# ScalarE and VectorE in place of GpSimd for the weight split of the plain projection stages

## What is computed

```python
def _ab_mixer(h, pos, s0, k_past, v_past, w_in, w_out, lam, lam_init, g_diff):
    qa, ka, va, ga, qb, kb, vb = jnp.split(h @ w_in, _cuts(AB_WIDTHS), axis=-1)
    qa = _rotary(qa.reshape(B, L, H_A, DK_A), pos)
...
def _gla_mixer(h, s0, w_in, w_gate, b_gate, g_norm, w_out):
    q, k, v, r, a = jnp.split(h @ w_in, _cuts(C_WIDTHS), axis=-1)
```

## Time and profile before

| | |
|---|---|
| median of 3 runs | 3545.07 us (3543.67 to 3548.8) |
| profiled execution | 3540.22 us |
| its span, first to last instruction | 3538.4 us |
| mean granted clock of TensorE | 0.940 of full speed |
| busy: PE / DVE / ACT / POOL | 3037.2 / 1540.1 / 1030.3 / 375.0 us |

### The profile page before, as it was taken

One profiled execution on the slowest core, in us unless ns is written; L12 is line 12 of the kernel. 1 busy time (PEld: TensorE's weight loads), 2 busy tenths in 40 slices (PEclk: granted clock), 3 DMA queues, 4 the chain that ended last, 5 costly groups with the idle time before them and its releaser, 6 DMA issues. The chain is left out here.

```text
span 3538.4 us, 52416 instructions
## 1 busy us (share of the span) xinstructions
PE 3037.2 (86%) x19700; PEld 2801.0 (79%) x19700; DVE 1540.1 (44%) x2144; ACT 1030.3 (29%) x1907; POOL 375.0 (11%) x281
## 2 busy tenths in 40 slices
PE   4699986788699999999984999767489999999996
PEld 2688874344499999999984989556288999999996
DVE  2144113556556444444446000287628444444545
ACT  4111111334444233322325101243225332333222
POOL 1212100000200000000001223163100000000000
PEclk8899997899799999999997999889789999999998
DMA  4354533775331111111103211121223111111113
GB/s 164 113 183 170 177 132 113 278 258 191 103 115 53 46 43 42 41 41 48 43 26 106 78 58 66 40 77 36 97 97 125 47 43 41 47 41 47 41 41 103
DMA packets 154186, 319.76 MB, mean 90 GB/s; under 512 B 12657, under 2 KB 86354, under 8 KB 145122
## 3 DMA queue, kind: packets, MB, share of 16 engines
q1 hardware_dynamic: 117314, 241.16, 20.2%
q10 hardware_dynamic: 36768, 77.21, 6.3%
HBM read 272.69 MB, written 45.64 MB: 90 GB/s over the span
## 5 line engine op out<-in xcount | busy, mean ns | idle before, releaser
L520 PE MATMUL f_acc<-m_hi,f_hi 128*128 128x352 f32 x1248 | 409.5, 328 | 42.8 <-DVE f_lo L1160 39.6
L520 PE MATMUL f_acc<-h_hi,f_hi 128*128 128x352 f32 x1248 | 409.4, 328 | 23.9 <-DVE f_lo L1160 20.7
L520 PE MATMUL f_acc<-h_hi,f_lo 128*128 128x352 f32 x1248 | 406.3, 326 | 0.0
L520 PE MATMUL f_acc<-m_hi,f_lo 128*128 128x352 f32 x1248 | 406.3, 326 | 0.0
L520 PE MATMUL f_acc<-h_lo,f_hi 128*128 128x352 f32 x1248 | 404.0, 324 | 0.0
L520 PE MATMUL f_acc<-m_lo,f_hi 128*128 128x352 f32 x1248 | 403.9, 324 | 0.0
L520 PE MATMUL f_acc<-f_ghi,f_hi 128*128 128x352 f32 x1056 | 346.2, 328 | 51.1 <-DVE y L1293 30.9
L1293 DVE TENSOR_TENSOR y<-y,f_acc 128x1056 f32<-128x1056 f32 x176 | 218.7, 1252 | 337.4 <-PE f_acc L520 337.4
L520 PE MATMUL f_acc<-f_glo,f_hi 128*128 128x352 f32 x1056 | 344.0, 326 | 0.0
L520 PE MATMUL f_acc<-f_ghi,f_lo 128*128 128x352 f32 x1056 | 343.9, 326 | 0.0
L1266 DVE SCALAR_TENSOR_TENSOR f_cv<-f_up,vec,f_cv 128x1072 f32<-128x1072 f32 x88 | 117.3, 1333 | 363.4 <-ACT f_cv L1130 363.4
(11 more groups left out here) (355 smaller groups left out, 5914.0 us busy)
## 6 DMA issues: line engine op xcount, KB each, us to landing
f_st<-w_ffn SPq DMA_DIRECT2D x132, 512.0 KB, 3.5
kt<-cache_k SPq DMA_DIRECT2D x128, 256.0 KB, 5.2
att_vt<-cache_v SPq DMA_DIRECT2D x128, 256.0 KB, 5.7
y<-w_ada ACTq DMA_DIRECT2D x20, 1024.0 KB, 5.1
qkv_ada_w<-w_ada ACTq DMA_DIRECT2D x20, 1024.0 KB, 5.2
y<-w_qkv SPq DMA_DIRECT2D x10, 1024.0 KB, 6.1
x<-y ACTq DMA_DIRECT2D x6, 1408.0 KB, 6.2
n_x<-x SPq DMA_DIRECT2D x12, 704.0 KB, 8.0
```

Of the source, the lines that this page charges most:

```text
L520: last = nc.tensor.matmul(out, a(kk), b(kk), start=(n == 0), stop=(n == 3 * nk - 1))
```

## The change

`split_first` and `split_units` are gone, and GpSimd has no code in the four stages. Every unit is now rounded by ScalarE (`round_unit`) and subtracted by VectorE (`rest_unit`). In all four stages the first two units are split ahead of everything else, so ScalarE's initial `taken` and `ready` counts now stand behind the rounding of the second unit. In `stage_linear` ScalarE rounds unit n+2 right behind taking unit n out of PSUM and ahead of its store. In `stage_project` ScalarE rounds the next pass's unit u behind its work on the last tile of this pass's unit u; VectorE subtracts unit 0 behind the rotation of tile 10 (`q == TILES + 1`) and unit 1 behind that of tile 17, ahead of the last modulation sum; in plain passes the subtractions stand behind the fifth and the eighth modulation sum. The last pass, or the last pair of units, is written out behind the loop, without roundings. In the FFN stages two helpers are only renamed. SyncE's and TensorE's code is the same.

```diff
--- before.py
+++ after.py
@@ -484,32 +484,17 @@
                                             ALU.mult).then_inc(hid, 1)
 
 
-def split_first(nc, act, dve, st, hi, lo, landed, made, chain):
-
-
-    if act is not None:
-        act.wait_ge(landed[0], 16)
-        nc.scalar.activation(hi[0][:], st[0][:], ACT.Copy).then_inc(chain, 1)
-    else:
-        dve.wait_ge(chain, 1)
-        nc.vector.tensor_tensor(lo[0][:], st[0][:], hi[0][:].bitcast(F32), ALU.subtract).then_inc(made, 1)
-
-
-def split_units(nc, pool, g, n_pairs, st, hi, lo, landed, made, freed, free_at, pool_chain):
-
-    def split(i, u):
-        pool.wait_ge(landed[u], i * 16 + 16)
-        pool.wait_ge(freed, free_at(i, u))
-        shape = [P, st[u].shape[1]]
-        nc.gpsimd.tensor_tensor(hi[u][:], st[u][:], bc(g.ones[:, 0:1], shape), ALU.mult).then_inc(pool_chain, 1)
-        pool.wait_ge(pool_chain, i * 2 + (u + 1))
-        nc.gpsimd.tensor_tensor(lo[u][:], st[u][:], hi[u][:].bitcast(F32), ALU.subtract).then_inc(made, 1)
-
-    pool.wait_ge(made, 1)
-    split(0, 1)
-    with pool.Fori(1, n_pairs) as i:
-        for u in range(2):
-            split(i, u)
+def round_unit(nc, act, st, hi, landed, landed_at, freed, freed_at, rounded):
+
+    act.wait_ge(landed, landed_at)
+    act.wait_ge(freed, freed_at)
+    nc.scalar.activation(hi[:], st[:], ACT.Copy).then_inc(rounded, 1)
+
+
+def rest_unit(nc, dve, st, hi, lo, rounded, rounded_at, made):
+
+    dve.wait_ge(rounded, rounded_at)
+    nc.vector.tensor_tensor(lo[:], st[:], hi[:].bitcast(F32), ALU.subtract).then_inc(made, 1)
 
 
 def three_passes(nc, out, whi, wlo, xhi, xlo, nk):
@@ -534,7 +519,7 @@
         lo = [k.sb(f"lo{i}", [P, UW], F32R) for i in range(2)]
         acc = [k.ps(f"acc{i}", [P, NT, 512]) for i in range(2)]
         landed = [k.sem(f"landed{i}") for i in range(2)]
-        made, used, taken, pc = k.sem("made"), k.sem("used"), k.sem("taken"), k.sem("pool")
+        made, used, taken, rounded = (k.sem(x) for x in ("made", "used", "taken", "rounded"))
         stored = k.sem("stored")
         block = stack.enter_context(nc.Block())
 
@@ -546,11 +531,6 @@
                 for u in range(2):
                     sp.wait_ge(made, i * 2 + (u - 1))
                     sp.dma_start(st[u][:], w[i * 2 + u]).then_inc(landed[u], 16)
-
-        @block.gpsimd
-        def _(pool):
-            split_units(nc, pool, g, n_units // 2, st, hi, lo, landed, made, used,
-                        lambda i, u: i * 2 + (u + 1), pc)
 
         @block.tensor
         def _(pe):
@@ -569,22 +549,35 @@
 
         @block.vector
         def _(dve):
-            split_first(nc, None, dve, st, hi, lo, landed, made, pc)
+            with dve.Fori(0, n_units // 2) as i:
+                for u in range(2):
+                    rest_unit(nc, dve, st[u], hi[u], lo[u], rounded, i * 2 + (u + 1), made)
 
         @block.scalar
         def _(act):
-            split_first(nc, act, None, st, hi, lo, landed, made, pc)
+            for u in range(2):
+                round_unit(nc, act, st[u], hi[u], landed[u], 16, used, u + 1, rounded)
             act.sem_inc(taken, 2)
             at = 0
+
+            def finish(i, at, evacuate, store, more):
+                for u in range(2):
+                    act.wait_ge(used, i * 2 + (u + 3))
+                    evacuate(i * 2 + (u - at), acc[u][:, :, 0:TT]).then_inc(taken, 1)
+                    if more:
+                        round_unit(nc, act, st[u], hi[u], landed[u], i * 16 + 32, used, i * 2 + (u + 3), rounded)
+                    if store is not None:
+                        act.wait_ge(taken, i * 2 + (u + 3))
+                        dst, src = store(i * 2 + (u - at))
+                        act.dma_start(dst, src).then_inc(stored, 16)
+
             for count, evacuate, store in sections:
-                with act.Fori(at // 2, (at + count) // 2) as i:
-                    for u in range(2):
-                        act.wait_ge(used, i * 2 + (u + 3))
-                        evacuate(i * 2 + (u - at), acc[u][:, :, 0:TT]).then_inc(taken, 1)
-                        if store is not None:
-                            act.wait_ge(taken, i * 2 + (u + 3))
-                            dst, src = store(i * 2 + (u - at))
-                            act.dma_start(dst, src).then_inc(stored, 16)
+                end = (at + count) // 2
+                final = at + count == n_units
+                with act.Fori(at // 2, end - 1 if final else end) as i:
+                    finish(i, at, evacuate, store, True)
+                if final:
+                    finish(end - 1, at, evacuate, store, False)
                 at += count
             n_stored = sum(count for count, _, store in sections if store is not None)
             if n_stored:
@@ -646,7 +639,7 @@
         acc = [k.ps(f"acc{i}", [P, 512]) for i in range(NR)]
         landed = [k.sem(f"landed{i}") for i in range(2)]
         stored = [k.sem(f"stored{i}") for i in range(NR)]
-        made, used, summed, pc = k.sem("made"), k.sem("used"), k.sem("summed"), k.sem("pool")
+        made, summed, rounded = k.sem("made"), k.sem("summed"), k.sem("rounded")
         ready, turned, copied = k.sem("ready"), k.sem("turned"), k.sem("copied")
         if n_rot:
             xc = k.sb("xc", [P, GW])
@@ -669,11 +662,6 @@
                 for u in range(2):
                     sp.wait_ge(made, i * 2 + (u - 1))
                     sp.dma_start(st[u][:], w[i * 2 + u]).then_inc(landed[u], 16)
-
-        @block.gpsimd
-        def _(pool):
-            split_units(nc, pool, g, passes, st, hi, lo, landed, made, summed,
-                        lambda i, u: i * DEPTH + (u + 1) * TILES, pc)
 
         @block.tensor
         def _(pe):
@@ -724,7 +712,12 @@
 
         @block.vector
         def _(dve):
-            split_first(nc, None, dve, st, hi, lo, landed, made, pc)
+
+            def rest(i, u):
+                rest_unit(nc, dve, st[u], hi[u], lo[u], rounded, i * 2 + (u + 1), made)
+
+            rest(0, 0)
+            rest(0, 1)
             if w_ada is not None:
                 ada.start_vector(dve)
             if n_rot:
@@ -751,12 +744,25 @@
                         dve.wait_ge(stored[q % NR], (i * (DEPTH // NR) + (q // NR + 1)) * 16)
                         dve.wait_ge(turned, i * DEPTH + (q + 1))
                         nc.vector.tensor_tensor(res[q % NR][0:r], xc[0:r], xs[0:r], ALU.add).then_inc(ready, 1)
+                        if q == TILES + 1:
+                            rest(i + 1, 0)
+                    rest(i + 1, 1)
                     if w_ada is not None:
                         ada.add(dve, i * UNITS + (UNITS - 1))
+
+            def plain_pass(i, more):
+                for c in range(UNITS):
+                    if w_ada is not None:
+                        ada.add(dve, i * UNITS + c)
+                    if more and c == UNITS // 2:
+                        rest(i + 1, 0)
+                if more:
+                    rest(i + 1, 1)
+
+            with dve.Fori(n_rot, passes - 1) as i:
+                plain_pass(i, True)
+            plain_pass(passes - 1, False)
             if w_ada is not None:
-                with dve.Fori(n_rot, passes) as i:
-                    for c in range(UNITS):
-                        ada.add(dve, i * UNITS + c)
                 dve.wait_ge(ada.added, passes * UNITS + 1)
                 chain = Seq(dve, ada_dv)
                 ada.finish(chain, 0, range(2, 6))
@@ -764,7 +770,12 @@
 
         @block.scalar
         def _(act):
-            split_first(nc, act, None, st, hi, lo, landed, made, pc)
+
+            def rounds(i, u):
+                round_unit(nc, act, st[u], hi[u], landed[u], i * 16 + 16, summed, i * DEPTH + (u + 1) * TILES, rounded)
+
+            rounds(0, 0)
+            rounds(0, 1)
             for s in range(NR):
                 act.sem_inc(stored[s], 16)
             act.sem_inc(copied, 2)
@@ -773,7 +784,7 @@
             if w_ada is not None:
                 ada.start_scalar(act)
 
-            def finish(i, rotate):
+            def finish(i, rotate, more):
                 if w_ada is not None:
                     for c in range(2):
                         ada.load(act, i * UNITS + c, c)
@@ -797,12 +808,15 @@
                         act.wait_ge(turned, i * DEPTH + (q + 1 + NR))
                         nc.scalar.activation(dst[:, bass.ds(i * 4 + 2 * u, 2), t * P:t * P + r],
                                              turn[q % 2][:, :, 0:r], ACT.Copy).then_inc(copied, 1)
+                    if more and t == TILES - 1:
+                        rounds(i + 1, u)
 
             if n_rot:
                 with act.Fori(0, n_rot) as i:
-                    finish(i, True)
-            with act.Fori(n_rot, passes) as i:
-                finish(i, False)
+                    finish(i, True, True)
+            with act.Fori(n_rot, passes - 1) as i:
+                finish(i, False, True)
+            finish(passes - 1, False, False)
```

## The result

| | before | changed |
|---|---|---|
| median (4 runs each) | 3544.37 us (3541.54 to 3548.8) | 3524.1 us (3518.61 to 3527.83) |
| ratio of the medians, 95% interval | | 0.994 [0.9923, 0.9958] |
| profiled execution | 3540.22 us | 3527.83 us |
| mean granted clock in it | 0.940 | 0.939 |

The changed kernel takes about 20 us less; 15.8 were forecast. By the ratio, 3545.07 x 0.994 is 3523.8 us, 0.2 us under the low end of the range; its interval allows 15 to 27 us. The direction and the mechanism (GpSimd's hold on VectorE's addition) were right.

What follows compares the result with a forecast made beforehand. TensorE bounds the kernel, idling in `qkv` where GpSimd holds up VectorE's SBUF addition. Terms -8.0 - 3.8 - 6.3 + 2.0 + 0.3 = -15.8 us take the median from 3545.07 to 3529.3 us; range 3524 to 3538.

Steps and rivals of the forecast that it cites:

- gaps at a pass's end: TensorE's 3.58 us idle at each of `qkv`'s three rotated pass ends shrinks to 0.92: -8.0 us.
- gaps in the middle: TensorE's waits in mid-pass of `qkv`'s rotated passes, 3.8 us in three pieces, all vanish: -3.8 us.
- the clock behind a pass's end: TensorE's lowered clock after each 3.58 us gap in `qkv` stays at full level instead: -6.3 us.
- the new chain: At `qkv` pass ends, copy, rounding, subtraction and rotation run in series; TensorE idles 1.0 us at two ends: +2.0 us.
- the stage starts (all four): TensorE's first matmul in each changed stage also waits for the second unit's rounding: +0.3 us for all.
- Rival A: Two short gaps per `qkv` pass end still lower the clock: only -9.5 us, 3535.6, at worst 3538; chance 0.14.
- Mid-pass, plain passes, linear stages: ScalarE's and VectorE's added steps stay hidden beside TensorE: 0 us, mid-pass up to +2 with 0.3 us of room.
- Rival C: Modulation loads queued behind ScalarE's second rounding land late at `qkv` pass ends: +16 us, 3561 us; chance 0.04.
- Outside `qkv`: GpSimd's other work and the other stages are untouched: 0 us; all stages but `qkv` shorter by nothing.

Runs made afterwards that it cites:

- e7: The changed kernel with VectorE's subtraction of the second unit done twice at each rotated pass's end in `qkv`; ratio to before 0.9968, `qkv` 335.6 us.
- e1: The changed kernel once more, unaltered, against the kernel before: 3522.91 us, ratio 0.9942.
- e10: The changed kernel run again, unaltered, against the kernel before: 3521.39 us, ratio 0.9945.
- e2: The kernel before with the change in `qkv` alone; `ga`, `vc` and `qkr` keep the old code: 3531.63 us, ratio 0.9963.
- e9: The change in `qkv` alone, timed a second time against the kernel before: 3526.37 us, ratio 0.9964.
- e6: The changed kernel, but in `qkv` GpSimd subtracts every unit but the first, behind ScalarE's rounding: 3526.24 us, ratio to before 0.9947.
- e3: The kernel before with the change in `ga`, `vc` and `qkr` only, `qkv` as before: 3541.25 us, ratio 0.9998.
- e4: The changed kernel plus unused GpSimd multiplications and subtractions of the old size in `qkv`'s first two rotated passes; ratio to before 0.9987, `qkv` 340.2 us.

## Why the prediction fell short

The mechanism was right. The step that failed is the sizing of three terms of the sum, of which two were wrong in opposite directions. By stretches (the table of turns above), forecast and measured, in `qkv`:

| term | forecast, us | measured, us |
|---|---|---|
| gaps at a pass's end | -8.0 | -8.0 |
| gaps in the middle | -3.8 | -4.3 |
| the clock behind a pass's end | -6.3 | -5.0 |
| the new chain | +2.0 | +0.4 |
| the stage starts (all four) | +0.3 | -1.3 (`qkv`'s) |
| all else | 0 | -0.2 |

**The gaps at a pass's end: right.** 2.66 us each was forecast as saved, and 0.9 as left. The row says 0.91.

**The gaps in the middle: right, and a little small.** None is left. The rows had 3.8 us of idle time; from turn to turn each pass gains 1.4 us, 4.3 in all, because an idle time of TensorE's row starts only at the end of the last record.

**The new chain: this step failed.** "Ready at T+6.8, wanted at T+5.8", +2.0 us for two ends. Measured from T = 233.63: the copy starts at T+0.59, not T+0.79 (the row it came from was at half clock, as the prediction had noted for its lower bound), and the rotation is done at T+6.45, not T+6.8. And TensorE comes for it not at T+5.8 but at T+6.3 (0.12 behind its matmul of 239.82). Its next product starts at 234.20: the turn takes 0.57 from start to start, for which I had put 0.2 ("an estimate, half of the 0.44"). The two products take 2.87 each from there on, close to the 2.80 that I had read from two of VectorE's rows. The turn starts at T+6.51. Two waits of 1.0 us became two of 0.2: 1.6 us of the gain that was missed. e7 fits: with 2.41 us more in the chain the wait grew by 2.41.

**The stage's start: this step failed too.** +0.3 us was put down as the cost of the second rounding in all four stages. That cost is nothing in `qkv`: the rounding was over at 165.40 against a start of 165.38. What I had not thought of is the clock. Over the stage's own first 5 us it was 0.67 instead of 0.50, in e1's trace 0.66 and in e10's 0.70, and the first turn comes 1.3 us earlier. Some 0.3 of this is the end of GpSimd's hold on the first addition (with the old `ga` and the new `qkv`, e2 and e9, it is 8.2 us); the other 1.0 goes with the clock. It is no chance of one execution: nine traces with the new `ga` have it, three with the old one don't (e9 and e10, above). The forecast has no term for it.

**The clock behind a pass's end: too large by 1.3 us.** It is 1.00 behind every one, as forecast. But of the 6.3 us only 5.0 are back: 1.3, 2.3 and 1.4 us, from a pass's last turn on and without the new waits of 0.2. Length x (1 - clock) takes for granted that all of the stretch goes faster at full clock. The way from the last turn to the next product does not: it was 0.60 us at half clock (239.16 to 239.76 before) and is 0.57 now. That is some 0.3 us for each end; the rest I can't name. With the new chain this makes -4.6 us where -4.3 was forecast. That these two came out in their sum is luck.

Rival A, and the Trainium skill's rule on frequent short idle times that would have chosen it ("TensorE: Matmul & The Clock Gate", section "A second HAM failure mode: psum-queue depth-cycling"), did not come about behind gaps of 0.9 us. The pair of short gaps that I was afraid of came as 0.91 and 0.2 us; e6 has it at 0.91 and 1.13, and its clock is 1.00 as well.

**Mid-pass, plain passes, linear stages: right**, 0 (e3 for the last two). In mid-pass the room was 0.7 us rather than 0.3.

**Rival C** had no occasion: the modulation's loads went out at 234.84 and 235.38, while the rounding ran and not behind it, and TensorE never waited for them.

**Outside `qkv`** the forecast was 0. The medians of the three comparisons differ by 20 to 21 us, `qkv` by 18.4, so about 2 us are in no term. The first traces have 1.4 of them in stretches with unchanged code, and no run shows their cause.

**The range failed on its low side.** It let the new wait go to nothing, but had no room for a gain beyond the terms, and gave 3 us for the runs' own spread. The kernel before had already spread over 5.1 us in three runs, and the changed one's four runs spread over 9.2. Attention alone, with the same code, takes from 280 to 292 us in the traces. That the result lies 0.2 us outside is less than any of this; that it lies near the edge at all comes from the terms above.

## What to carry to other kernels

A small VectorE operation with two inputs in SBUF that takes several times what its sisters with a PSUM input take, and ends with a GpSimd instruction, is a hold: find the GpSimd instruction, and give it to ScalarE where that has room, first of all where TensorE has nothing behind the held operation. Look for the same pattern in the whole program, since here the stages that the change had not touched gave another 19 us. And where a step stands behind such a place, count the other engine's arrival instruction by instruction before booking a new wait: here 1.0 us twice was booked, and 0.2 came. Read such a wait from start to start, and in the row of the weight load: the matmul's row showed none. Before a window of one trace is compared with that of another, start both at the same instruction: `qkv` starts at 165.4 us in one trace of the changed kernel and at 167.2 in the next.

## What the runs showed of the hardware

GpSimd's hold on VectorE's operations with two inputs in SBUF was seen for additions (from 0.41 to as much as 3.3 us), for the subtraction of a weight unit (from 2.29 to 3.66 in e4) and for SCALAR_TENSOR_TENSOR (a pair from 2.55 to 5.99). One with an input in PSUM went on at 0.41 us beside GpSimd.

The granted clock fell to 0.66 for 5 us behind an idle time of TensorE of 2.41 us, with 6.5 us of work between it and a gap of 0.91. It did not fall behind 0.91 (the changed kernel), behind 1.24 us, or behind 1.13 and 1.20 with a gap of 0.91 the same 6.5 us ahead (e6). What lies between 1.24 and 2.41 is not shown.

What I had not expected is how much a stage of many short matmuls varies by itself: attention took 279.8, 281.2, 281.4, 283.3, 283.5, 283.7, 285.8, 286.2, 290.7, 290.8, 290.9 and 292.4 us in the traces of this study, with the same code. The clock in it was 0.91 to 0.93 where it took up to 286.2, and 0.87 to 0.90 where it took 290.7 or more. One profiled execution can so hide or feign 10 us; the stage times show which.
